# A two-block model on one core: separate buffers for the RWKV keys, chunk loads issued during the gate units, and a retention stage with its heads written out

## The reference, cut to what matters

```python
# RWKV-7: six mixes of u with u shifted by a token; products; a normalised key
mixes = u[None] + (shifted - u)[None] * mu[:, None, None, :]
r, k, v, g = jnp.einsum("pbsd,pdw->pbsw", mixes[:4], w_in)
decay = jnp.exp(-jnp.exp(-jax.nn.softplus(-(w0 + jnp.tanh(mixes[4] @ w1) @ w2)) - 0.5))
iclr = jax.nn.sigmoid(a0 + (mixes[5] @ a1) @ a2)
kk = heads(k * k_k); kk = kk / jnp.maximum(jnp.linalg.norm(kk, axis=-1, keepdims=True), 1e-12)
k = heads(k * (1.0 + (iclr - 1.0) * k_a))
# recurrence over tokens with r, decay, k, v, -kk, kk * iclr; group norm; times silu(g); @ w_out

# retention of one direction, chunks of 128 tokens, 4 heads (64 wide keys, 128 wide values)
inner = jnp.einsum('bhnd,bhmd->bhnm', qi, ki) * decay_intra
out = jnp.einsum('bhnm,bhmv->bhnv', inner, vi) + jnp.einsum('bhnd,bhdv->bhnv', qi * q_dec, R)
R = R * chunk_dec + jnp.einsum('bhmd,bhmv->bhdv', ki * k_dec, vi)
# q, k are rotated first; forward and backward are summed; o * rsqrt(mean(o * o)) * silu(gate)
```

## Time and profile before

| | |
|---|---|
| median of three runs (lowest to highest) | 3883.31 us (3881.01 to 3886.58) |
| the profiled execution's own time | 3878.87 us |
| its span, first to last instruction | 3877.1 us |
| PE busy | 3420.5 us (88%) |
| DVE, ACT, POOL busy | 1853.0 (48%), 1387.1 (36%), 693.2 (18%) |

### The profile page before, as it was taken

The page is one execution under the profiler, slowest core; times in us unless marked ns, Lnnn a source line. Parts: engine busy times, 40 slices in busy tenths (PEclk is TensorE's granted clock), DMA queues, the critical chain, the costliest instruction groups (busy, mean ns, idle before and its releaser), DMA issues. The chain is left out here.

```text
span 3877.1 us, 74722 instructions
## 1 busy us (share of the span) xinstructions
PE 3420.5 (88%) x32138; PEld 2120.4 (55%) x32138; DVE 1853.0 (48%) x2539; ACT 1387.1 (36%) x2002; POOL 693.2 (18%) x422
## 2 busy tenths in 40 slices
PE   6978999969798697989998899978799999888889
PEld 3335766644343244888887466645544466545434
DVE  3654566552424533545554456633352366623352
ACT  3553445432454431333333435532211255512111
POOL 2000000020000001333332033322260133132330
PEclk8989999979899798999999999999999999999999
DMA  5101101031243443111111221010012211020121
GB/s 157 33 21 53 39 27 38 22 109 33 76 98 93 105 117 105 42 60 51 51 60 40 66 73 49 7 53 28 14 55 71 60 38 33 1 64 17 41 76 44
DMA packets 308035, 215.19 MB, mean 56 GB/s; under 512 B 125379, under 2 KB 283918, under 8 KB 305166
## 3 DMA queue, kind: packets, MB, share of 16 engines
q1 hardware_dynamic: 307320, 210.70, 18.1%
q10 hardware_dynamic: 442, 0.37, 0.0%
HBM read 173.26 MB, written 41.98 MB: 56 GB/s over the span
## 5 line engine op out<-in xcount | busy, mean ns | idle before, releaser
L140 PE MATMUL psum<-u,w_hi 128*128 128x512 f16 x2816 | 857.0, 387 | 101.9 <-DVEq L796 32.1
L140 PE MATMUL psum<-u,w_lo 128*128 128x512 f16 x1408 | 542.6, 385 | 0.0
L140 PEld LDWEIGHTS psum<-u,w_hi 128*128 128x128 f16 x2816 | 279.6, 100 | 451.4 <-issue 57.5
L97 POOL TENSOR_TENSOR w_hi<-stage,w_scale 128x1024 f16<-128x1024 f32 x76 | 144.9, 1907 | 1157.3 <-PE psum L2258 414.1
L1061 PE MATMUL psum<-w_hi,merged 128*128 128x512 f16 x768 | 235.9, 389 | 25.0 <-PEq L2790 9.1
L2468 DVE CUSTOM_DVE_ANT_0 probs_att<-psum,bias_att 128x1024 f32<-128x1024 f32 x128 | 156.7, 1225 | 168.2 <-PE psum L2280 167.7
L2258 PE MATMUL psum<-u,w_hi 128*128 128x512 f16 x768 | 231.4, 383 | 6.3 <-PEq L964 6.3
L140 PEld LDWEIGHTS psum<-u,w_lo 128*128 128x128 f16 x1408 | 140.0, 99 | 173.2 <-issue 12.5
L1061 PE MATMUL psum<-held_hi_out,merged 128*128 128x512 f16 x768 | 231.0, 379 | 0.0
L115 DVE SCALAR_TENSOR_TENSOR w_lo<-stage,w_hi 128x1024 f16<-128x1024 f32 x100 | 120.0, 1220 | 135.2 <-ACT w_hi L109 135.0
L101 POOL TENSOR_TENSOR w_lo<-stage,w_hi 128x1024 f16<-128x1024 f32 x76 | 177.3, 2333 | 10.8
(11 more groups left out here) (441 smaller groups left out, 6815.4 us busy)
## 6 DMA issues: line engine op xcount, KB each, us to landing
stage<-w_in SPq DMA_DIRECT2D x72, 512.0 KB, 3.8
X<-rwkv_chunks SPq DMA_DIRECT2D x16, 1792.0 KB, 7.6
stage<-ab_w_in SPq DMA_DIRECT2D x48, 512.0 KB, 5.1
rwkv_chunks<-work_rp SPq DMA_DIRECT2D x44, 512.0 KB, 5.6
stage<-rw_w_in SPq DMA_DIRECT2D x32, 512.0 KB, 5.0
stage<-w_out SPq DMA_DIRECT2D x24, 512.0 KB, 5.6
X<-x SPq DMA_DIRECT2D x16, 512.0 KB, 10.9
stage<-ab_w_out SPq DMA_DIRECT2D x16, 512.0 KB, 5.3
```

The lines of the kernel that those rows point to most:

```text
L97: pool.tensor_tensor(K.w_hi[:, slot, :], K.stage[:, slot, :], scale, ALU.mult).then_inc(K.w_half[slot], 1)
L140: last = pe.matmul(K.psum[:, bank, :], w[:, k, :], u[:, k, cols], start=(k == 0 and n == 0), stop=(k == KT - 1 and n == 2))
```

## The change

Four pieces, of one commit.

1. `channel_major` gets an optional semaphore: the very first unit of `rwkv_project` waits for each channel tile of its mix in turn instead of for all eight.
2. In the k units, KK gets three buffers of its own (`yb`), the step value one (`step`), BE is written in place over `iclr`, and K is stored by itself. ACT then waits for `k_ready` (DVE is done with the unit two back) where it waited for the stores. The KK and BE of a unit are stored one unit late.
3. The gate's array is moved last in `rwkv_chunks`; its products go to buffers in `u32`. After the fourth gate unit SP waits for every earlier store and loads the first two chunks without the gate. `rwkv_chunks` waits for the gate stores itself and loads the missing part; its waits for the constants stand later.
4. In `retention` the loops are gone. The first two rotations are made ahead of the fourth unit, the other two inside head 0; the norm of a head stands behind the next head's values; ACT and DVE split the weights, and POOL has no work there.

```diff
-def channel_major(pe, K, slot, rnd, u_hi, u_lo, banks):
+def channel_major(pe, K, slot, rnd, u_hi, u_lo, banks, tile_ready=None):
...
+            if half == 0 and tile_ready is not None:
+                pe.wait_ge(tile_ready, k + 1)
...
-R_, K_, V_, G_, KK_, BE_, SG_ = range(RW_ARRAYS)
+R_, K_, V_, KK_, BE_, SG_, G_ = range(RW_ARRAYS)
...
-        beb = [work[n] for n in (4, 7)]
+        yb = [work[n] for n in (8, 9, 7)]
+        step = work[4]
-        t1b = [work[n] for n in (8, 9)]
...
+                def keys(j):
+                    sp.wait_ge(k_ready, j + 1)
+                    sp.dma_start(scratch[KK_, j], chunked(yb[j % 3])).then_inc(kk_stored[j % 3], 16)
+                    sp.dma_start(scratch[BE_, j], chunked(iclr[:, j, :])).then_inc(be_stored, 16)
...
                     elif m == 1:
-                        sp.wait_ge(k_ready, j + 1)
-                        for arr, b in ((K_, kp), (KK_, kkb), (BE_, beb)):
-                            sp.dma_start(scratch[arr, j], chunked(b[j % 2])).then_inc(k_stored[j % 2], 16)
+                        sp.wait_ge(taken, n + 1)
+                        sp.dma_start(scratch[K_, j], chunked(kp[j % 2])).then_inc(k_stored[j % 2], 16)
+                        if j:
+                            keys(j - 1)
...
                         sp.wait_ge(taken, n + 1)
-                        sp.dma_start(scratch[G_, j], chunked(ob[j % 4])).then_inc(stored[j % 4], 16)
+                        sp.dma_start(scratch[G_, j], chunked(gb[j % 4])).then_inc(chunk.gate_stored[j % 4], 16)
+                        if j == 3:
+                            all_but_gate()
+                            for p in range(2):
+                                sp.dma_start(chunk.raw[:, p, 0:G_], A["scratch"][p, :, 0:G_]).then_inc(chunk.raw_in[p], 16)
...
                         if j >= 2:
-                            act.wait_ge(k_stored[j % 2], 48 * (j // 2))
-                        else:
-                            for b in stored:
-                                act.wait_ge(b, 32)
+                            act.wait_ge(k_ready, j - 1)
+                        elif j == 0:
+                            act.wait_ge(stored[1], 32)
...
                 def key(j):
...
+                    if j < 2:
+                        dve.wait_ge(stored[3 * j], 32)
+                    else:
+                        dve.wait_ge(k_stored[s2], 16 * (j // 2))
...
-                load(0, 0)
-                load(1, 1)
+                for stored in chunk.gate_stored:
+                    sp.wait_ge(stored, 32)
+                for p in range(2):
+                    sp.dma_start(raw[:, p, G_], A["scratch"][p, :, G_]).then_inc(gate_in[p], 16)
...
+                for n in range(3):
+                    channel_major(pe, K, n, first_round, K.u_hi, K.u_lo, (2 * n, 2 * n + 1))
+                pe.wait_ge(consts_in, 16 * 9)
+                cross(0)
+                cross(1)
+                channel_major(pe, K, 3, first_round, K.u_hi, K.u_lo, (6, 7))
+                for hd in range(H):
+                    double(hd)
+                    if hd == 0:
+                        cross(2)
+                    values(hd)
+                    if hd:
+                        norm(hd - 1)
+                    score(hd)
+                    turn(hd)
+                    if hd == 0:
+                        cross(3)
+                    delta(hd)
+                    channel_major(pe, K, *slot_of(hd, 1), K.u_hi, K.u_lo, (0, 1))
+                    output(hd)
+                norm(H - 1)
```

More of the change, by code:

```diff
@@ L1296, in rwkv_project @@
         k_stored = [sem(f"k_stored{n}") for n in range(2)]
+        kk_stored = [sem(f"kk_stored{n}") for n in range(3)]
+        be_stored = sem("be_stored")
         toks = lambda t: slice(t * P, (t + 1) * P)
@@ L1979, in gate @@
                 def gate(c, q):
+                    if not after(c, 1):
+                        pool.wait_ge(gate_in[q], 16)
                     pool.tensor_tensor(wg[:, q], raw[:, q, G_], cols("ln_w"), ALU.mult)
@@ new lines, in _ @@
+                for n in range(3):
+                    take_raw(n)
+                act.wait_ge(gamma_ready, 1)
+                decays(0)
+                take_raw(3)
+                for hd in range(H):
+                    unit_done(act, K, *slot_of(hd, 0))
+                    act.mul(v[:, :, :].rearrange("p t c -> p (t c)"), PROJ, UNSCALE).then_inc(v_ready, 1)
+                    if hd:
+                        rstd(hd - 1)
+                    act.wait_ge(k2_done, hd + 1)
+                    act.copy(k2_turned[:, :, :].rearrange("p t c -> p (t c)"), K.bank_pair(2)).then_inc(k2_ready, 1)
+                    if hd:
+                        high_part(hd - 1)
+                    split_high(act, K, *next_unit(hd, 0))
+                    unit_done(act, K, *slot_of(hd, 1))
+                    act.activation(gate[:, :], PROJ, ACT.Sigmoid, scale=UNSCALE).then_inc(g_sig, 1)
+                    act.preload_act_table_set("natural_log_exp_and_others")
+                    act.wait_ge(out_done, hd + 1)
+                    if hd:
+                        act.wait_ge(low_ready, hd)
+                    act.activation(sq[:, :], OUT, ACT.Square)
+                    act.copy(O[:, :], OUT).then_inc(o_taken, 1)
+                    if hd + 1 < H:
+                        decays(hd + 1)
+                        split_high(act, K, *next_unit(hd, 1))
@@ new lines, in _ @@
+                distances(0)
+                for n in range(3):
+                    split_low(dve, K, n, first_round + 1)
+                rotate(0)
+                rotate(1)
+                split_low(dve, K, 3, first_round + 1)
+                for hd in range(H):
+                    decayed(hd)
+                    if hd:
+                        split_low(dve, K, *next_unit(hd - 1, 1))
+                    else:
+                        rotate(2)
+                    dve.wait_ge(scores_done, hd + 1)
+                    dve.tensor_tensor(scores[:, :, :], chunks(K.bank_pair(1)), spread(near[:, :]),
+                                      ALU.mult).then_inc(scores_taken, 1)
+                    if hd == 0:
+                        rotate(3)
+                    if hd:
+                        gated(hd - 1)
+                    states(hd)
+                    if hd + 1 < H:
+                        dve.drain()
+                        distances(hd + 1)
+                    if hd:
+                        low_part(hd - 1)
+                    split_low(dve, K, *next_unit(hd, 0))
+                    dve.wait_ge(g_sig, hd + 1)
+                    dve.scalar_tensor_tensor(gate[:, :], PROJ, UNSCALE, gate[:, :],
+                                             ALU.mult, ALU.mult).then_inc(g_taken, 1)
```

303 lines of the change are left out of this document (156 added, 147 removed).

## The result

The changed kernel takes 3753.1 us (median of 4 runs, 3749.03 to 3758.37); the kernel before takes 3882.16 us beside it. The ratio is 0.9668, with a 95% interval of 0.9651 to 0.9685: 129 us faster. A second set of five runs gave 3757.5 us against 3882.29 (ratio 0.9675, 0.9661 to 0.9688), 125 us. The forecast was 3758.6 us, a gain of 124.7.

A forecast was written before the change was run, and what follows sets the result against it. PE was busy 88% of the span, so only its waits could be won. Gains of 5.5 (first r unit), 43.7 (k units), 9.9 (border) and 65.6 (retention) sum to 124.7: 3883.3 - 124.7 = 3758.6 us, range 3744 to 3785.

The forecast's parts named there:

- The first r unit: Start of the projections: PE starts tile by tile instead of waiting for all eight mix tiles; gain 5.5 us.
- The k units: Key projection: stores drop out of ACT's turn, 12.9 us instead of 20.2, DVE's chain leading; six waits gain 43.7 us.
- The stores' cover: k units: each unit's DMA, 2.1 MB at 288 to 318 GB/s, takes some 7.5 us, 58% of a 12.9 us turn.
- The border: Behind the g units: it waits only for DVE's split, so the decay sum starts at 1510.4 instead of 1520.22; gain 9.9 us.
- Retention: Two retention stages: each falls to 210.1 us from 242.5 and 243.3, heads 1 to 3 taking 36.2 each; gain 65.6 us.
- The tail: Retention's end, last output to pooling's first product: 14.4 us before, plus 0.9 for O's copy and 1.1 for a split: 16.4.
- The splits: Retention: 12 per stage on ACT and DVE, covered except the last; rival, on the path, 3794 us, chance 0.09.
- The signs: Trace signs of a wrong prediction: ACT or DVE ending head waits, k turns over 14 us, untouched stages moving over a few us.
- The rivals: Stores lead again (0.07), k turn unshortened (0.03), border's data late (0.05), splits on retention's path (0.09), slower, PE program supply (0.02).

The follow-up runs named there:

- the run with the clamp: Changed kernel with tile waits in all four first units, splits on POOL in retention, DVE's clamp of the previous unit ahead of the key product: 3730.4 us.
- the run with POOL: Changed kernel with POOL splitting the weights in retention again, and ACT and DVE not: 3748.5 us.

## Why the prediction was right

The mechanisms were right, piece by piece. That the stages' sum came within 0.2 us, 124.9 for 124.7, is partly luck: 2.2 us that were not in the sum (the starts of v and g) stood against 2.1 lost in retention and at the border. The time of the whole kernel moves more than that from one set of runs to the next (gains of 129 and 125 us).

- **The first r unit**: 5.5 forecast, 5.8 measured.
- **The k units**: a turn of 12.9 forecast, 12.99 measured; the gain 43.7 and 43.5. The cause is confirmed by putting the wait back, and the leader, DVE, by the run with the clamp. I took the whole 7.3 us a turn for the wait; with the wait put back 6.0 of it return, and 1.2 do not, which I put down to the earlier store of K. PE's idle time ahead of v was to be about 14 us and is 9.47. The 14 did not follow from my own terms: 106.7 us of k units less eight turns of 12.1 leave 10.
- **The stores' cover**: right in effect; too high in its rate. 288 GB/s held in a burst, not in a steady stream.
- **The border**: 9.9 forecast (9.8 by its own terms, 1520.22 less 1510.4), 9.4 measured. The decay sum starts 2.45 us behind DVE's last split, as worked out; the chain from there is 9.87 us and not 9.47. Of its DVE operations the decay sum takes 1.68 us instead of 2.31, the two differences 1.52 and 1.37 instead of 1.30 and 0.69. POOL's first two products ran beside this chain before too, but now beside other operations of it; that they cause the change is likely and not shown.
- **The starts of v and g**: not in the sum, 0.8 and 1.4 us. The first unit of v takes 12.2 us instead of 13.0, at a granted clock of 0.85 instead of 0.80, behind a wait of 9.47 us instead of 19.96.
- **Retention**: the heads 36.2 forecast, 36.0 measured. Head 0 ends at 84.9, forecast 85.1. The tail is 17.7 instead of 16.4: the last norm's sums take 3.56 us at a granted clock of 0.54, where I had 1.98 (clock 1.00 in the trace before). The wait inside heads 1 to 3 is the one named, 1.10; head 0 has 1.41 where I had 1.2 for DVE's product.
- **The splits**: I counted 1.1 us for them in the tail, which came, 1.2. What they cost the stages behind retention was in no term: 2.3 us against the kernel before, 3.6 against the run with POOL.
- **The signs**: two of those that I named are badly worded. "ACT or DVE ends the waits inside a head" would call the prediction wrong, though ACT ends the 1.10 us and DVE the 1.41 that my own sum contains. And the stages that no piece touches did move, 2.9 us within their spread and 2.3 by retention's new form; "a few us" cannot tell one from the other.
- **What the parts of retention are worth**: the norm's order 13.2 and the early rotations 7.5 us of 32.0 a stage, by the runs; the splits' move -1.2. That leaves 12.5. The rotation of the second pair was not tried alone. By its rows it is most of the rest: before, PE spent 13.1 us between the starts of these two rows, and the doubling then took 5.82 us instead of 3.60; now there are two products of 1.75 us and a wait of 1.41 in head 0, 0.3 more than in the others. That is an estimate of 11.5 us.

```profile
2702.61 5.39 PE L2665 MATMUL psum<-merged,swap_ret 128*128 x8 [2.43 <-ACT sq_ret L2708]
...
2715.67 5.82 PE L2622 MATMUL psum<-rot_ret,twice_ret 128*128 128x512 f32 x8 [7.67 <-DVE rot_ret L2745]
```

- **The rivals**: none came. PE ran the written-out program at full pace; the values' unit takes 10.8 us as in the loop.

## What to carry to other kernels

Price a removed wait by the next chain that closes the loop, engine by engine; here that gave 12.9 us for 12.99, and named the engine to shorten next. When a unit's first product waits for all tiles of its operand, let it wait tile by tile: three more such places gave 16 us for one line. Before moving work off an engine that looks slow, ask whether anything waits for it: in the new order nothing did, and taking the splits off POOL cost some 6 us, most of it in stages that the change does not touch. So compare the neighbours of a changed stage in several traces, and not the stage alone.

## What was not expected of the hardware

- Pieces of 256 B against long ones: stores 288 against 414 to 430 GB/s, loads 217 against mostly 401 to 459.
- The same stores in 256 B pieces ran at 288 to 291 GB/s while ACT and DVE waited for them, and at 200 to 230 in part of the turn when they were spread over it. No run here separates the causes.
- The g units start behind a wait of 3.32 us in both kernels. Before, the first of them had a clock of 0.88 and took 11.9 us, after, 1.00 and 10.5 us, with PE fully busy at 1.00 ahead of the wait in both. These are the rows of both; no run here explains the difference.

```profile
1420.10:1432.00 11.90, 11.90 (x49) 5.13 (x50) 1.06 (x1) 0.92 (x1) 0.00 (x0) 0.88 0.35 88
```

```profile
1369.30:1379.80 10.50, 10.50 (x49) 4.78 (x50) 1.04 (x1) 0.90 (x1) 0.00 (x0) 1.00 0.41 100
```
